# A decoder trunk on one core: attention's and the linear attention's small matmuls joined into fewer groups on TensorE, some of them later

## What is computed

```python
u = rms_norm(x, norm1_w[l])
proj = u @ w_in[l]
(cx, cb, cc, gq, gk, gv, gr, ga, sq, sk, sv, gates) = jnp.split(proj, split_idx, axis=-1)
ya = short_conv_mixer(cx, cb, cc, conv_w[l], conv_b[l])
yb = gla_mixer(gq, gk, gv, gr, ga, gla_wa2[l], gla_ba[l], gla_onorm_w[l])
yc = swa_mixer(sq, sk, sv, positions, q_norm_w[l], k_norm_w[l], sinks[l])
...
x = x + mixed @ w_o[l]
h = rms_norm(x, norm2_w[l])
x = x + jnp.square(jax.nn.relu(h @ w_up[l])) @ w_down[l]
```

## Time and profile before

| | |
|---|---|
| time, median of 3 runs | 1600.87 us (1600.61 to 1601.12) |
| profiled execution: its time | 1601.0 us |
| profiled execution: span of the trace | 1598.9 us |
| TensorE matmul busy | 1582.3 us, 99% |
| TensorE weight load busy | 1298.8 us, 81% |
| VectorE busy | 1011.4 us, 63% |
| ScalarE busy | 723.3 us, 45% |
| time of the packets, share of 16 DMA engines | 28.0% for the main queue |

### The profile page before, as it was taken

How to read it: one execution, slowest core, us unless ns; L and a number is a source line. 1 busy time by engine, 2 the same in 40 slices (tenths; PEclk the granted TensorE clock), 3 DMA queues, 4 the chain that set the end, 5 groups by cost and what they waited for, 6 DMA issues and landing times.

```text
span 1598.9 us, 21070 instructions
## 1 busy us (share of the span) xinstructions
PE 1582.3 (99%) x7536; PEld 1298.8 (81%) x7536; DVE 1011.4 (63%) x1430; ACT 723.3 (45%) x1108; POOL 0.2 (0%) x4
## 2 busy tenths in 40 slices
PE   7999999999999999999999999999999999999999
PEld 5878778888888888888888777788888888888887
DVE  5576774455556869696346677645455578787952
ACT  5547552223346464545345475522233474636350
POOL 0000000000000000000000000000000000000000
PEclk9999999999999999999999999999999999999999
DMA  5321222233361232324022212123323514141401
GB/s 152 130 80 53 80 80 80 79 112 99 107 210 53 100 112 87 125 75 141 6 74 90 94 42 93 53 80 116 121 79 106 184 54 158 53 158 53 152 7 53
DMA packets 108166, 151.11 MB, mean 95 GB/s; under 512 B 4992, under 2 KB 81312, under 8 KB 108064
## 3 DMA queue, kind: packets, MB, share of 16 engines
q1 hardware_dynamic: 107632, 149.69, 28.0%
q10 hardware_dynamic: 432, 0.08, 0.0%
HBM read 147.67 MB, written 2.10 MB: 94 GB/s over the span
## 4 chain that ended last, share of the span: by engine, by line
PE 94%; DVE 3%; ACT 1%; DMA 1%; DVEq 0%; issue 0%; SPq 0%; ACTq 0%
PE acc L535 19%; PE acc L537 19%; PE acc L536 19%; PE acc L557 6%; PE acc L559 6%; PE acc L558 6%; PE acc L586 5%; PE acc L588 5%; PE acc L587 5%; PE bank L726 1%; PE bank L745 1%; DVE wl_rows L1039 1%; PE bank L737 1%; PE bank L603 1%; DMA raw<-in_w_in_dram 1%; PE bank L684 1%
## 5 line engine op out<-in xcount | busy, mean ns | idle before, releaser
L535 PE MATMUL acc<-uh,wh 128*128 128x512 f32 x1152 | 453.2, 393 | 2.9 <-DVEq L1056 2.4
L537 PE MATMUL acc<-uh,wl 128*128 128x512 f32 x1152 | 448.7, 389 | 0.0
L536 PE MATMUL acc<-ul,wh 128*128 128x512 f32 x1152 | 448.6, 389 | 0.0
L535 PEld LDWEIGHTS acc<-uh,wh 128*128 128x128 f32 x1152 | 216.3, 188 | 55.0 <-issue 5.4
L822 ACT ACTIVATE wh<-raw 128x1024 fp32r<-128x1024 f32 x142 | 150.5, 1060 | 232.2 <-PE acc L537 156.5
L537 PEld LDWEIGHTS acc<-uh,wl 128*128 128x128 f32 x1152 | 216.3, 188 | 45.6
L536 PEld LDWEIGHTS acc<-ul,wh 128*128 128x128 f32 x1152 | 216.4, 188 | 43.5
L1039 DVE TENSOR_TENSOR wl<-raw,wh 128x1024 fp32r<-128x1024 f32 x142 | 174.0, 1225 | 82.4 <-ACT wh L822 71.0
L822 ACT ACTIVATE wh_rows<-raw_down 128x1024 fp32r<-128x1024 f32 x100 | 106.2, 1062 | 134.8 <-PE acc L588 35.6
L1039 DVE TENSOR_TENSOR wl_rows<-raw_down,wh_rows 128x1024 fp32r<-128x1024 f32 x100 | 122.5, 1225 | 58.2 <-ACT wh_rows L822 50.8
L1065 DVE TENSOR_TENSOR gate_tanh<-acc,rsqrt_rows 128x512 f32<-128x512 f32 x48 | 33.2, 691 | 116.2 <-PE acc L537 116.0
(11 more groups left out here) (227 smaller groups left out, 2464.0 us busy)
## 6 DMA issues: line engine op xcount, KB each, us to landing
raw<-in_w_in_dram SPq DMA_DIRECT2D x39, 1024.0 KB, 5.0
raw<-in_w_up_dram SPq DMA_DIRECT2D x32, 1024.0 KB, 5.8
raw_down<-in_w_down_dram SPq DMA_DIRECT2D x32, 1024.0 KB, 8.3
raw_branch<-in_w_in_dram SPq DMA_DIRECT2D x12, 1024.0 KB, 4.9
raw_branch<-in_w_branch_dram SPq DMA_DIRECT2D x12, 1024.0 KB, 5.0
raw_branch<-in_w_o_dram SPq DMA_DIRECT2D x8, 1024.0 KB, 5.0
x_tokens<-in_x_dram SPq DMA_DIRECT2D x8, 256.0 KB, 5.6
raw_kv<-in_w_in_dram SPq DMA_DIRECT2D x4, 512.0 KB, 3.6
```

Of the source, the lines that this page charges most:

```text
L535: nc.tensor.matmul(a[:], wh[slot][:, k, :], right_h, start=at_k == 0, stop=False)
L536: nc.tensor.matmul(a[:], wh[slot][:, k, :], right_l, start=False, stop=False)
L537: last = nc.tensor.matmul(a[:], wl[slot][:, k, :], right_h, start=False, stop=at_k == n - 1)
```

## The change

Only the two lists `PE_ORDER` and `ACT_ORDER` change. No instruction is added, removed or resized, `DVE_ORDER` stays, and every small step takes the same bank as before, since their order among themselves is the same. What moves is their place among the big matmuls:

- `UT1` joins `UT0` ahead of `gk0.0`; `UT2` and `UT3` stand ahead of `gk1.0` and no longer behind it.
- `KD` stands behind `gv3.3` (the last six matmuls of `gv3`), with `QT0`; `QT2` joins `ATT1` and `QT1`; `SC0` and `QT3` stand six matmuls later.
- `PT0` moves six matmuls later to join `KV1`; `PV0` no longer stands with it and comes 18 matmuls after; `SC3` moves six later and joins `GO0`; `GO1` and `PV1` move behind the whole of `cx0`.
- `SC6`, `YT2` and `PV4` move behind `cb0` (24 matmuls) and so join `PT5` and `YT3`.
- `PV6` moves behind `gate0.0` (12 matmuls) and joins `PT7`.
- On ScalarE, `ss0` stands behind `UT1`, and `ss1` to `ss3` behind `UT3`.

```diff
-PE_ORDER = """gq0.0 gq1.0 UT0 gk0.0 UT1 gk1.0 UT2 UT3 gq0.1 gq1.1 NROW gk0.1 gk1.1 kva0 kva1 kva2 kva3 sq0.012 AT sq0.3 sq1.0 ZA
+PE_ORDER = """gq0.0 gq1.0 UT0 UT1 gk0.0 UT2 UT3 gk1.0 gq0.1 gq1.1 NROW gk0.1 gk1.1 kva0 kva1 kva2 kva3 sq0.012 AT sq0.3 sq1.0 ZA
...
-cx2.0 PV2 cx2.1 cx3 cc0.0 PT3 SC4 cc0.1 PV3 SC5 YT0 cc1 cc2 cc3.0 YT1 PT4 cc3.1 SC6 YT2 PV4 cb0 PT5 YT3 cb1.0 SC7 PV5
+cx2.0 PV2 cx2.1 cx3 cc0.0 PT3 SC4 cc0.1 PV3 SC5 YT0 cc1 cc2 cc3.0 YT1 PT4 cc3.1 cb0 SC6 YT2 PV4 PT5 YT3 cb1.0 SC7 PV5
...
-ACT_ORDER = """+gk1 UT0 ss0 UT1 ss1 UT2 ss2 UT3 ss3 +kva0 +kva1 attz +kva2 +kva3 +sq0 +sq1 +sq2 kva0 kva1 kva2 kva3 +sq3 +gv0 ZA +gv1
+ACT_ORDER = """+gk1 UT0 UT1 ss0 UT2 UT3 ss1 ss2 ss3 +kva0 +kva1 attz +kva2 +kva3 +sq0 +sq1 +sq2 kva0 kva1 kva2 kva3 +sq3 +gv0 ZA +gv1
```

More of the change, by code:

```diff
@@ L59, in pieces_of @@
     return unit, [int(c) for c in some] if some else list(whole)
-PE_ORDER = """gq0.0 gq1.0 UT0 gk0.0 UT1 gk1.0 UT2 UT3 gq0.1 gq1.1 NROW gk0.1 gk1.1 kva0 kva1 kva2 kva3 sq0.012 AT sq0.3 sq1.0 ZA
-sq1.123 sq2 sq3 gv0 gv1.01 KT0 gv1.23 gv2 gv3.012 KT1 ATT0 KD gv3.3 QT0 gr0.0 ATT1 QT1 gr0.1 QT2 gr0.2 SC0 QT3 gr0.3
-gr1.01 SC1 KV0 gr1.23 PT0 gr2.01 KV1 PV0 gr2.23 gr3.0 PT1 SC2 gr3.12 SC3 gr3.3 GO0 cx0.0 GO1 PV1 cx0.1 cx1.0 PT2 cx1.1
-cx2.0 PV2 cx2.1 cx3 cc0.0 PT3 SC4 cc0.1 PV3 SC5 YT0 cc1 cc2 cc3.0 YT1 PT4 cc3.1 SC6 YT2 PV4 cb0 PT5 YT3 cb1.0 SC7 PV5
-cb1.1 cb2 PT6 cb3 PV6 gate0.0 PT7 gate0.1 gate1.0 PV7 gate1.1 gate2 gate3""".split()
-ACT_ORDER = """+gk1 UT0 ss0 UT1 ss1 UT2 ss2 UT3 ss3 +kva0 +kva1 attz +kva2 +kva3 +sq0 +sq1 +sq2 kva0 kva1 kva2 kva3 +sq3 +gv0 ZA +gv1
+PE_ORDER = """gq0.0 gq1.0 UT0 UT1 gk0.0 UT2 UT3 gk1.0 gq0.1 gq1.1 NROW gk0.1 gk1.1 kva0 kva1 kva2 kva3 sq0.012 AT sq0.3 sq1.0 ZA
+sq1.123 sq2 sq3 gv0 gv1.01 KT0 gv1.23 gv2 gv3.012 KT1 ATT0 gv3.3 KD QT0 gr0.01 ATT1 QT1 QT2 gr0.23 SC0 QT3
+gr1.01 SC1 KV0 gr1.23 gr2.0 PT0 KV1 gr2.123 PV0 gr3.0 PT1 SC2 gr3.123 SC3 GO0 cx0 GO1 PV1 cx1.0 PT2 cx1.1
+cx2.0 PV2 cx2.1 cx3 cc0.0 PT3 SC4 cc0.1 PV3 SC5 YT0 cc1 cc2 cc3.0 YT1 PT4 cc3.1 cb0 SC6 YT2 PV4 PT5 YT3 cb1.0 SC7 PV5
+cb1.1 cb2 PT6 cb3 gate0.0 PV6 PT7 gate0.1 gate1.0 PV7 gate1.1 gate2 gate3""".split()
+ACT_ORDER = """+gk1 UT0 UT1 ss0 UT2 UT3 ss1 ss2 ss3 +kva0 +kva1 attz +kva2 +kva3 +sq0 +sq1 +sq2 kva0 kva1 kva2 kva3 +sq3 +gv0 ZA +gv1
 +gv2 sq0 sq1 sq2 sq3 ZB +gv3 KT0 +gr0 +gr1 +gr2 gv0 gv1 KT1 gv2 KD +gr3 gv3 QT0 QT1 QT2 QT3 +cx0 SC0 SM0 SC1 +cx1 PT0
```

## The result

| | median | range |
|---|---|---|
| before | 1600.86 us | 1600.61 to 1601.47, 6 runs |
| changed | 1607.12 us | 1605.73 to 1607.90, 6 runs |

The ratio is 1.0038, with a 95% interval of 1.0026 to 1.0050. The change costs 6.3 us where 1.5 was forecast; the time lies outside the range, whose upper end was 1606.5. The profiled execution took 1606.06 us, with a span of 1603.9 against 1598.9.

A forecast was written before the change was run, and what follows sets the result against it. The prediction took TensorE, busy for 99% of the span, to bound the kernel. Gains of 3.4, 2.1 and 0.6 us against a loss of 7.6 gave +1.5, so 1602.4 us, with 1599.8 to 1606.5 holding 8 in 10.

The forecast's parts named there:

- What bounds the kernel: TensorE, busy 99% of the span; three waits of 2.4, 2.1 and 0.5 us, about 5 us, cap gains from waits.
- Step 1: UT0 to UT3 and the square sums, at the start of a layer: a gain of 3.4 us.
- Step 2: KD behind gv3.3: its wait for VectorE's rotation goes whole, a gain of 2.1 us.
- the signs: What the trace would show: waits of about 3.8 us twice at YT3, none at KD, KD's group about 3 us earlier.
- Step 3: Fewer seams between TensorE's groups: a gain of 0.6 us over two layers, between 0 and 1.0.
- Step 4: YT3 behind YT2 without cb0 between waits for its bank: 3.8 us a layer, a loss of 7.6 us.
- the sum: All terms for the whole kernel added plainly: -3.4 - 2.1 - 0.6 + 7.6 = +1.5 us.
- the first rival: The clock falls in the new wait at YT3, slowing matmuls: 3.0 us more for two stretches, 1605.4; chance 0.17.
- the bank was not free in time: Rival that YT3's bank is free in time, so the 7.6 us loss vanishes: 1594.8 us; chance 0.10.
- no gain was handed on: Rival that NROW takes back all 3.4 us gained at the layer's start: 1605.8 us; chance 0.13.

The follow-up runs named there:

- The other moves alone: The kernel before with only the moves of QT2, SC0, PT0, PV0, SC3, GO1 and PV6 to their new places: 1600.90 us (1.0001).
- the filled wait: The changed kernel with 12 matmuls of 128x512 more in each layer ahead of YT3, adding nothing to the result: 1602.59 us (1.0011).
- the kernel with that part alone: The kernel before with only SC6, YT2 and PV4 moved behind cb0: 1610.92 us (1.0063).

## Why the prediction was wrong

- **What bounds the kernel**: right that the time is TensorE's. Of the three waits that I read, the two that the change aims at went; the third, at a weight's low part, stayed (0.2 us in the profile of the changed kernel, 0 to 0.9 in the others). The 5 us of waits were not quite the cap that I called them: the two waits read 4.5 us together, and removing them gained 5.4, since the view counts idle time from the modelled end of a matmul, which lies 0.16 us behind the place of the next one (0.39 less 0.23).
- **Step 1**, gain of 3.4 us: right, 3.3 alone. `ss3` was to start at 26.6 and `NROW` at 31.1 in layer 0; in the changed kernel they started here:

```profile
26.79 1.06 ACT L837 ACTIVATE squares_x<-x_tokens 128x1024 f32<-128x1024 f32 x1 [0.17 <-issue]
...
31.29 0.62 PE L611 MATMUL bank<-consts,rsqrt_tokens 128*128 128x128 f32 x4 [0.17 <-DVEq L1205]
```

- **Step 2**, gain of 2.1: right for the change, but not for the reason I gave. I wrote that the banks of what is queued behind are ready "as they were". They are so only because `ATT1` moved too; without that some 0.8 us comes back there. In the signs I put `KD`'s group about 3 us earlier than 100.2; it came at 98.36, 1.8 earlier, which is what step 1's gain of 1.95 in layer 0 says.
- **Step 3**, seams 0.6: too much, though within its bounds of 0 and 1.0. The other moves alone saved nothing that can be seen, and the join at `YT3` saves 0.1 a layer and not 0.2. The three steps together gained 5.4 (the kernel with the `YT3` part undone), against 5.7 forecast for them, which is 6.1 less the 0.4 of that part's seam. (`PV0`, which I called 18 matmuls later, stands 12 later than before and 18 behind `KV1`, which moved six earlier; no wait came of it.)
- **Step 4**, the wait: its mechanism and place were right, and its price nearly so. I had 7.6 less 0.4 of seams; the filled wait shows 7.2, which is 3.7 us less a seam of 0.1, twice. The two terms were too large by about as much, so that the exact 7.2 is in part luck. Had the clock held, the kernel would take 1602.6, and the forecast was 1602.4.
- **The step that failed** is the sum's silence on the clock: behind the wait at `YT3` it has no term for slower matmuls, which puts that at nothing, and it measured 4.5 us. 1602.4 and 4.5 make 1606.9, against 1607.12 measured. I had the mechanism as the first rival, gave it 0.17, and argued that the wait is half as long as the one at the start, and that groups of small matmuls slow nothing behind them. Neither speaks against it: all 14 waits of 3.5 us that have a profile (six executions of the changed kernel, one of the kernel with that part alone) are followed by a low stretch, and even waits of 2.1 us are in some runs. The rival's 1605.4 already said "slower" by more than can be mistaken, which is what came.
- **Its price** was too small as well. I took 1.5 us a wait from the transposes at the start, whose slow pace lasts 3.25 us. But the clock may fall before the wait ends and stay low for nearly all of the 12 big matmuls behind it; then it is 2.7 or 2.8 us. Over single waits I find 1.3 to 2.8, so 2.9 to 5.4 for both, 4.5 at the median. With 3.0 for both the rival gave 1605.4, and the range ended at 1606.5. An upper bound could be read from rows 8: all 12 matmuls of `cb1.0` at twice their spacing of 0.23, 2.8 us more, and `YT3`'s four transposes at twice 0.44, 0.4 more.
- The Trainium skill, "TensorE: Matmul & The Clock Gate", section "Why this matters for your kernels", which the prediction cites, says that an idle gap between bursts of matmuls brings the clock down. The traces agree, by 0.50 granted behind 3.5 us of standing still, and in some runs behind 2.1.
- **The other rivals** did not come: the bank was not free in time, and no gain was handed on but the 0.2 us at `NROW` that step 1 had in it.

## What to carry to other kernels

Before joining groups of small steps, count how far apart two uses of the same buffer come to stand, and on which engine the release is queued: a ring of four banks needs work that covers the slowest reader's whole queue (here `SC6` and a weight's low part, 6.8 us), and the work that covers it must stand between the two uses, not ahead of both. Price a new wait of TensorE twice, once for its length and once for the half-speed matmuls behind it, up to all that stand there; here the second price was six tenths of the first. And a saved seam is worth 0.2 us at most by the starts, and the joins tested alone saved nothing that can be seen, while one uncovered bank cost 11.7 us over two layers, so it is the waits that pay for such a reordering.

## What the runs showed of the hardware

- Standing still for 3.5 us, behind 3.3 us of small matmuls, was followed by the low level in each profiled case, 14 of 14; by their times, three runs without a profile had it behind one of their two waits only. Behind 2.1 us it came in some runs and not in others of the same program: in one of four profiled waits, and by their times at least once in 7 of 11 and 8 of 11 runs. Waits of 1.1 us, as in the kernel before, were not followed by one: behind the wait at 29.39 the matmuls start 0.23 us apart with a granted clock of 1.00, and its times stay within 1600.5 and 1601.6 in every series.
- When the clock falls, and what that costs, differs from execution to execution: during the wait (0.73 and 0.85 granted in its last 2 us), or a microsecond and more after TensorE is back at work (0.98, then 0.50). The two low stretches together cost 2.9 to 5.4 us in the same program, with both waits at 3.5 us. Kernels with waits of 2.1 or 3.5 us measured with a spread of 2.2 to 3.6 us, those without with 0.5 to 1.3.
- At the start of the kernel before, the transposes ran at 203 ns each while the granted clock reads 1.00; in the middle of the program the clock's column and the spacing of matmuls agree (0.50 with 0.43 us, 1.00 with 0.23). Why the column misses the start isn't known.
